# Prompt attention, two heads a step: turned copies ahead of newer exponentials on ScalarE, and the probabilities scaled on GpSimd

## The chip, the cores and the metric

The kernel runs on one core of one Trainium2 chip. The time is that of one execution on the device in microseconds, and the number given for a kernel is the median of its runs.

## The reference, cut to what matters

One step of a decoder with one layer, for 512 prompt tokens and 32 sample tokens. The part that the change touches is the attention of the prompt tokens: 8 heads of latent attention (queries and keys of 96 values, causal) and 8 heads of dilated window attention (64 values). The kernel treats the three dilations of the second kind as one softmax whose scores carry the logarithm of how many windows hold the key. Both kinds then read as follows, per head and per block of 128 queries:

```python
s = q @ k.T * scale + mask          # 128 queries x up to 512 keys
p = exp(s - max(s)); p = p / sum(p) # softmax_stats
o = p @ v
```

The rest of the layer (projections, attention of the sample tokens over cached pages, feed-forward network, gated embedding) stands before and after, and is not changed.

## The kernel before

Everything is laid out with features on the partitions and tokens along the free dimension, in float32. Each engine has a program of its own, written out by hand, and all order between engines comes from semaphores: an engine that waits holds up everything behind it in its program.

**The units.** The prompt attention is a list of 32 units, `units = [(p, i)]`: `p` is a pair of heads (0 to 7; 0 to 3 are latent heads, 4 to 7 window heads) and `i` a block of 128 queries (0 to 3). Unit (p, i) has (i + 1) x 128 keys, so its tiles are 128, 256, 384 and 512 wide, and then it starts again at 128. Each operation on a unit is done for its two heads (z = 0, 1). I call the four units of a pair "the 128, 256, 384 and 512 unit". The eight pairs are numbered 0 to 7.

**The stages of unit n, and who does them.**

1. *Scores*, TensorE, L1012, into one of two PSUM pairs (ps0, ps3).
2. *Masked scores and row maximum*, VectorE, L1273, one instruction and a short read of the accumulator for each head, PSUM to the buffer `probs_of(n, z)` in SBUF; three units have buffers (the names `att` and `prHigh`). Then the negated maximum, L1277 (semaphore `a_nm`).
3. *Exponentials* in place with the row sums, ScalarE, L739, two instructions with an accumulator read each (semaphore `a_e`).
4. *Reciprocal* of the sums, VectorE, L1281, and *scaling* of the probabilities in place by it, VectorE, L1285, twice (semaphore `a_p`).
5. *Turning*: 128x128 blocks are transposed by TensorE through the identity, L1022, into the one PSUM pair ps1 (semaphore `a_t`).
6. *Copy of the turned blocks* for both heads, ps1 to SBUF, one instruction on ScalarE, L748, into `prT` (even units) or a part of `ring` (odd units) (semaphore `a_tc`).
7. *Product with the values*, TensorE, L1033 (semaphore `a_pv`); after a 512 unit VectorE copies the pair's result out, L1291.

**The order of each engine.** At step n TensorE does scores of n, turning of n - 2, product of n - 3. VectorE does stage 2 of n, then stage 4 of n - 1. ScalarE does the exponentials of n and behind them the copy of n - 2. Since ps1 is single, the turning of a unit waits for the copy of the unit before it as well as for its own scaled probabilities. At a few steps other work is put in between: a split of a weight (L752, L1295, steps 6 and 7), clearing and laying out of the sample queries on VectorE (L1297 to L1315, steps 8, 10, 12), and on TensorE the absorbed sample queries (L984, step 24) and the sample tokens' scores among themselves (L993 to L998, step 26) with their read by VectorE.

**GpSimd** has in this stretch only the issue of eight large copies in DRAM (L639, `copy_v`), each held back until the scores of the units 0, 4, 8 and so on are started.

Of the kernel before, what the change touches and what calls it, by code (L numbers as in the profile page):

```python
# [34 lines left out]
P = 128  # L35
# [71 lines left out]
def build(nc, x, cst, gains, win, wqb, wk, wv, wkt, wo, wgu, wdn, wdn2, wpl, plt, pgt, pgl, ck, cv, pt,  # L107
          y, o_lat, o_kr, o_ks, o_vs, o_ck, o_cv):
    with ExitStack() as ctx:
# [18 lines left out]
        def sem(name):  # L128
            return ctx.enter_context(nc.semaphore(name))
# [86 lines left out]
            "krope_spread", "latnew_mm", "latnew_ev", "knew_sq", "knew_ssq"))  # L216
        p_nr = sem("new_scores_read")
        a_s, a_sm, a_e, a_p, a_t, a_tc, a_pv, a_o, a_nm = (sem(n) for n in (
# [409 lines left out]
        def _(pool):  # L628
# [34 lines left out]
            pool.wait_ge(out_s, 80)  # L663
            for k in range(8):
                pool.wait_ge(a_s, 8 * k + 1)
                copy_v(k // 2, k % 2)

# [7 lines left out]
        def _(act):  # L675
# [56 lines left out]

            for n in range(len(units) + LAG_T):
                if n < len(units):
                    w = (units[n][1] + 1) * P
                    act.wait_ge(a_nm, n + 1)
                    for z in range(2):
                        pr = probs_of(n, z)[:, 0:w]
                        last = act.activation(pr, pr, ACT.Exp, bias=st[:, n % 3, NEGM, z:z + 1],  # L739
                                              accum_out=st[:, n % 3, SUM, z:z + 1])  # L740
                    last.then_inc(a_e, 1)
                if n >= LAG_T:
                    m = n - LAG_T
                    w = (units[m][1] + 1) * P
                    act.wait_ge(a_t, m + 1)
                    if m >= 2:
                        act.wait_ge(a_pv, m - 1)
                    act.activation(prT[m % 2][:, :, 0:w], ps[1][:, :, 0:w], ACT.Copy).then_inc(a_tc, 1)  # L748
                if n == 6:
# [442 lines left out]
        def _(v):  # L1192
# [50 lines left out]
            for n in range(len(units) + LAG_PV + 1):  # L1243
# [34 lines left out]
                if 1 <= n <= len(units):  # L1278
                    m = n - 1
                    v.wait_ge(a_e, m + 1)  # L1280
                    link(v.reciprocal(st[:, m % 3, REC1, :], st[:, m % 3, SUM, :]))  # L1281
                    w = (units[m][1] + 1) * P
                    for z in range(2):
                        pr = probs_of(m, z)[:, 0:w]
                        last = v.tensor_scalar(pr, pr, st[:, m % 3, REC1, z:z + 1], None, ALU.mult)  # L1285
                    last.then_inc(a_p, 1)
                if n >= LAG_PV + 1:
# [327 lines left out]
```

## Time and profile before

| | |
|---|---|
| median of 3 runs | 1310.25 us (1310.02 to 1311.48) |
| the profiled execution's own time | 1311.06 us |
| its span in the profile | 1309.3 us |
| TensorE busy | 1204.9 us, 92% |
| VectorE, ScalarE, GpSimd busy | 581.0, 478.6 and 45.7 us |
| the 32 units of prompt attention | about 341.5 to 459.3 us |
| TensorE, VectorE, ScalarE, GpSimd busy in that stretch | 98.7, 74.0, 61.3 and 4.1 us of 117.8 |

In the profile PE is TensorE, PEld its weight loads, DVE VectorE, ACT ScalarE, POOL GpSimd. A float32 matmul stands as several records. The rows give the start and the duration in us, then engine, line, operation, what is written and read, and in brackets how long the engine was idle before it and what ended that. The starts of neighbouring instructions on one engine can be closer together than their durations, because they overlap in the pipeline.

### The profile page before, as it was taken

The numbers are of one execution on the slowest core, as the hardware profiler recorded it, in microseconds if no ns is written. First come the engines' busy times: TensorE is split into PE (matmuls) and PEld (weight loads), VectorE is DVE, ScalarE is ACT, GpSimd is POOL, SyncE is SP. The second block draws the span as 40 slices with busy tenths as digits, with TensorE's granted clock in tenths as the row PEclk, the third lists the DMA queues.
The fourth block names the chain that finished last, engine by engine and source line by source line (L and its number), as shares of the span: only waits on it lengthen the run. The fifth ranks groups of instructions, "written<-read, shape, count | busy, mean of one in ns | idle before, by whom it ended". The sixth has DMA issues, their size and how long they took to land.

```text
span 1309.3 us, 21517 instructions
## 1 busy us (share of the span) xinstructions
PE 1204.9 (92%) x8308; PEld 1007.5 (77%) x8308; DVE 581.0 (44%) x1031; ACT 478.6 (37%) x829; POOL 45.7 (3%) x60
## 2 busy tenths in 40 slices
PE   4999989999988799999999789799999999999698
PEld 3997977333556576666677478799999999999698
DVE  4313321453575576666666364632333233333643
ACT  4223233211355455555555432433321122222332
POOL 0000000232000000000000000000000000000000
PEclk8999999976788799999999879899999999999899
DMA  6675413002348247777777112364662354562122
GB/s 235 237 257 177 139 46 92 10 1 87 129 161 292 71 137 243 245 244 234 247 231 217 48 49 98 113 222 147 216 227 95 136 210 159 208 226 100 43 78 88
DMA packets 68815, 202.66 MB, mean 155 GB/s; under 512 B 7457, under 2 KB 40226, under 8 KB 67394
## 3 DMA queue, kind: packets, MB, share of 16 engines
q1 hardware_dynamic: 66562, 131.74, 30.9%
q0 software_dynamic: 2176, 69.90, 14.9%
q8 instruction: 48, 0.79, 0.2%
q14 instruction: 29, 0.24, 0.1%
HBM read 196.53 MB, written 72.13 MB: 205 GB/s over the span
## 4 chain that ended last, share of the span: by engine, by line
PE 86%; DVE 8%; ACT 3%; issue 2%; DMA 0%; SPq 0%; DVEq 0%; ACTq 0%
PE ps L497 50%; PE ps L1045 13%; PE ps L390 4%; PE ps L401 3%; PE ps L1012 2%; PE ps L413 2%; PE ps L1022 2%; PE ps L1033 2%; DVE R L438 2%; DVE tmp L455 1%; PE ps L1102 1%; PE ps L1096 1%; DVE aLo L356 1%; PE ps L1061 1%; PE ps L936 1%
## 5 line engine op out<-in xcount | busy, mean ns | idle before, releaser
L497 PE MATMUL ps<-aHi,wHi 128*128 128x272 f32 (+1 forms) x1392 | 296.0, 294 | 38.5 <-DVE aLo L356 35.1
L497 PE MATMUL ps<-aHi,wLo 128*128 128x272 f32 (+1 forms) x1392 | 291.8, 292 | 0.0
L497 PE MATMUL ps<-aLo,wHi 128*128 128x272 f32 (+1 forms) x1392 | 291.1, 291 | 0.0
L497 PEld LDWEIGHTS ps<-aHi,wHi 128*128 128x128 f32 (+1 forms) x1392 | 220.0, 189 | 48.9 <-issue 19.5
L369 DVE TENSOR_TENSOR wLo<-ring,wHi 128x1024 fp32r<-128x1024 f32 (+3 forms) x105 | 133.4, 1271 | 211.5 <-ACT wHi L364 211.4
L497 PEld LDWEIGHTS ps<-aLo,wHi 128*128 128x128 f32 (+1 forms) x1392 | 221.2, 190 | 0.0
L497 PEld LDWEIGHTS ps<-aHi,wLo 128*128 128x128 f32 (+1 forms) x1392 | 220.2, 190 | 0.0
L364 ACT ACTIVATE wHi<-ring 128x1024 fp32r<-128x1024 f32 (+3 forms) x105 | 114.5, 1091 | 196.1 <-PE ps L497 196.1
L1328 DVE TENSOR_REDUCE ssq<-att 128x8 f32<-128x512 f32 x128 | 87.4, 683 | 89.1 <-ACT att L767 88.3
L767 ACT ACTIVATE att<-ps 128x512 f32<-128x512 f32 x128 | 76.4, 597 | 114.6 <-PE ps L1045 114.0
L1045 PE MATMUL ps<-wkHi,pgHi 128*128 128x512 f32 x256 | 103.2, 403 | 8.2 <-ACT att L767 7.0
L1045 PE MATMUL ps<-wkHi,pgLo 128*128 128x512 f32 x256 | 100.0, 390 | 0.0
L1045 PE MATMUL ps<-wkLo,pgHi 128*128 128x512 f32 x256 | 99.7, 390 | 0.0
L497 PE MATMUL ps<-hidHi,wLo 128*128 128x272 f32 x352 | 72.9, 288 | 0.0
L497 PE MATMUL ps<-hidHi,wHi 128*128 128x272 f32 x352 | 72.7, 288 | 0.0
L497 PE MATMUL ps<-hidLo,wHi 128*128 128x272 f32 x352 | 72.5, 288 | 0.0
L390 PE MATMUL ps<-sq,C 128*128 128x272 f32 (+5 forms) x196 | 59.3, 456 | 14.1 <-ACT sq L298 14.1
L1045 PEld LDWEIGHTS ps<-wkHi,pgHi 128*128 128x128 f32 x256 | 48.1, 188 | 22.5 <-issue 12.3
L1412 DVE TENSOR_TENSOR sq<-ps,tmp 128x544 f32<-128x544 f32 x22 | 16.0, 725 | 101.3 <-ACT tmp L828 101.3
L390 PEld LDWEIGHTS ps<-sq,C 128*128 128x128 f32 (+5 forms) x196 | 25.6, 146 | 43.0 <-issue 21.7
L1045 PEld LDWEIGHTS ps<-wkHi,pgLo 128*128 128x128 f32 x256 | 48.1, 188 | 10.5
L497 PEld LDWEIGHTS ps<-hidHi,wHi 128*128 128x128 f32 x352 | 55.4, 188 | 0.0
(190 smaller groups left out, 1419.8 us busy)
## 6 DMA issues: line engine op xcount, KB each, us to landing
out_o_cv<-in_cv POOLq DMA_DIRECT2D x16, 2044.0 KB, 8.2
ring<-in_wgu SPq DMA_DIRECT2D x44, 512.0 KB, 3.5
big<-in_pgt SPq DMA_DIRECT2D x128, 144.0 KB, 2.2
big<-in_pgl SPq DMA_DIRECT2D x128, 128.0 KB, 2.4
kv<-in_ck SPq DMA_DIRECT2D x8, 1792.0 KB, 8.0
ring<-in_win SPq DMA_DIRECT2D x21, 512.0 KB, 4.4
kv<-in_cv SPq DMA_DIRECT2D x8, 1024.0 KB, 5.8
kv<-in_cv SPq DMA_DIRECT2D x24, 256.0 KB, 6.2
```

Of the source, the lines that this page charges most:

```text
L364: nc.scalar.activation(wHi[:, u % 2, 0:width], ring[:, u % 2, 0:width], ACT.Copy).then_inc(w_hi, 1)
L369: nc.vector.tensor_tensor(wLo[:, u % 2, 0:width], ring[:, u % 2, 0:width], wHi[:, u % 2, 0:width].bitcast(F32), ALU.subtract).then_inc(w_l ...
L390: last = nc.tensor.matmul(ps[2][out, a, 0:hw], ones, sq[rows, k % 2, a * hw:(a + 1) * hw], start=(j == 0 and t == 0), stop=(j == len(q["sr ...
L401: last = nc.tensor.matmul(spread_pair(g)[rows, a, 0:hw], C[src, C_W + t * P + rows.start:C_W + t * P + rows.stop], R[src, p % 2, a * hw:(a ...
L413: last = nc.tensor.matmul(ps[1][rows, a, 0:HT], C[rows, q["rope"][0] + rows.start:q["rope"][0] + rows.stop], q["dst"][0][:, a * HT:(a + 1) ...
L438: nc.vector.reciprocal(R[rows, p % 2, 0:w], R[rows, p % 2, 0:w]).then_inc(n_rc, 1)
L497: ins = nc.tensor.matmul(pair[rows, a, 0:HT], w[:, c], xx[:, k, a * HT:(a + 1) * HT], start=(k == 0 and z == 0), stop=(k == nk - 1 and z = ...
L767: act.activation(sqK[:, g % 2, :], ps[0][:, g % 2, :], ACT.Square).then_inc(k_sq, 1)
L1012: mm(score_pair(place(n))[:, z, 0:(i + 1) * P], q[:, i * P:(i + 1) * P], k[:, 0:(i + 1) * P], start=True, stop=True).then_inc(a_s, 1)
L1022: last = pe.transpose(ps[1][:, z, j * P:(j + 1) * P], probs_of(m, z)[:, j * P:(j + 1) * P], cm(C_ID))
L1045: last = mm(ps[0][:, g % 2, :], x_[:, g % NBUF, c * P:(c + 1) * P], w_[:, c, :], start=(c == 0 and z == 0), stop=(c == KC - 1 and z == 2))
L1328: v.tensor_reduce(ssq[:, b % 2, t * H:(t + 1) * H], sqK[:, g % 2, :].rearrange("p (h d) -> p h d", h=H), AX.X, ALU.add).then_inc(k_ss, 1)
```

## The change

Two edits, both within the 32 units.

On ScalarE the two blocks of the loop change places: at step n the copy of the turned blocks of unit n - 2 stands in front of the exponentials of unit n, where it stood behind them.

On VectorE the two scaling instructions of stage 4 are gone; the reciprocal stays and now raises a new semaphore `att_recip`. GpSimd scales: it waits for that semaphore, does the two `tensor_scalar` of the unit and raises `a_p`, which TensorE waits for as before. Its eight DRAM copies are spread among the units, each in front of the scaling of a 128 unit.

```diff
@@ gpsimd
-            for k in range(8):
-                pool.wait_ge(a_s, 8 * k + 1)
-                copy_v(k // 2, k % 2)
+            for n in range(len(units)):
+                if n % 4 == 0:
+                    pool.wait_ge(a_s, 2 * n + 1)
+                    copy_v(n // 8, n // 4 % 2)
+                w = (units[n][1] + 1) * P
+                pool.wait_ge(a_rc, n + 1)
+                for z in range(2):
+                    pr = probs_of(n, z)[:, 0:w]
+                    last = pool.tensor_scalar(pr, pr, st[:, n % 3, REC1, z:z + 1], None, ALU.mult)
+                last.then_inc(a_p, 1)
@@ scalar
             for n in range(len(units) + LAG_T):
+                if n >= LAG_T:
+                    m = n - LAG_T
+                    w = (units[m][1] + 1) * P
+                    act.wait_ge(a_t, m + 1)
+                    if m >= 2:
+                        act.wait_ge(a_pv, m - 1)
+                    act.activation(prT[m % 2][:, :, 0:w], ps[1][:, :, 0:w], ACT.Copy).then_inc(a_tc, 1)
                 if n < len(units):
                     w = (units[n][1] + 1) * P
                     act.wait_ge(a_nm, n + 1)
@@
                     last.then_inc(a_e, 1)
-                if n >= LAG_T:
-                    m = n - LAG_T
-                    w = (units[m][1] + 1) * P
-                    act.wait_ge(a_t, m + 1)
-                    if m >= 2:
-                        act.wait_ge(a_pv, m - 1)
-                    act.activation(prT[m % 2][:, :, 0:w], ps[1][:, :, 0:w], ACT.Copy).then_inc(a_tc, 1)
@@ vector
                     v.wait_ge(a_e, m + 1)
-                    link(v.reciprocal(st[:, m % 3, REC1, :], st[:, m % 3, SUM, :]))
-                    w = (units[m][1] + 1) * P
-                    for z in range(2):
-                        pr = probs_of(m, z)[:, 0:w]
-                        last = v.tensor_scalar(pr, pr, st[:, m % 3, REC1, z:z + 1], None, ALU.mult)
-                    last.then_inc(a_p, 1)
+                    v.reciprocal(st[:, m % 3, REC1, :], st[:, m % 3, SUM, :]).then_inc(a_rc, 1)
```

**ScalarE, one pair of heads (pair 3).** The rows are the program's order on that engine, before, and then of the change. L739 (L753 in the change) are the exponentials, x2 for two heads; L748 (L747) the copies of the turned blocks; the last number is the width.

```order
L739 ACTIVATE att,st<-att,st 128x256 x2
L748 ACTIVATE ring<-ps 128x2x512
L739 ACTIVATE prHigh,st<-prHigh,st 128x384 x2
L748 ACTIVATE prT<-ps 128x2x128
L739 ACTIVATE att,st<-att,st 128x512 x2
L748 ACTIVATE ring<-ps 128x2x256
L739 ACTIVATE att,st<-att,st 128x128 x2
```

```order
L747 ACTIVATE ring<-ps 128x2x512
L753 ACTIVATE att,st<-att,st 128x256 x2
L747 ACTIVATE prT<-ps 128x2x128
L753 ACTIVATE prHigh,st<-prHigh,st 128x384 x2
L747 ACTIVATE ring<-ps 128x2x256
L753 ACTIVATE att,st<-att,st 128x512 x2
```

The copy of the 256 unit (`ring<-ps 128x2x256`) stood behind the exponentials of the 512 unit and now stands in front of them; so does each other copy against the exponentials of the unit two further on.

**VectorE, the end of the same pair.** The ISA rows are the masked scores with their maximum, each followed by the read of its accumulator; L1277 (L1284) is the negated maximum, L1281 (L1288) the reciprocal of the unit before it, L1285 the scaling of that unit, L1291 (L1293) the copy of a finished pair. First before, then the change.

```order
L1273 ISA att,st<-ps,C 128x512
L1273 ISA st 128x1
L1277 TENSOR_SCALAR st<-st 128x2
L1281 RECIPROCAL st<-st 128x2
L1285 TENSOR_SCALAR att<-att,st 128x384 x2
L1291 COPY aT<-ps 128x512
```

```order
L1280 ISA att,st<-ps,C 128x512
L1280 ISA st 128x1
L1284 TENSOR_SCALAR st<-st 128x2
L1288 RECIPROCAL st<-st 128x2
L1293 COPY aT<-ps 128x512
```

The scaling is gone; the reciprocal of the 384 unit keeps its place behind the masked scores of the 512 unit.

**GpSimd, the first two pairs.** L639 is the issue of a DRAM copy, L672 the scaling, x2 for the two heads. These are rows of the change; before, the eight L639 stood here in a row with nothing between them.

```order
L639 DMA out_o_cv<-in_cv 32x16352
L672 TENSOR_SCALAR att<-att,st 128x128 x2
L672 TENSOR_SCALAR att<-att,st 128x256 x2
L672 TENSOR_SCALAR prHigh<-prHigh,st 128x384 x2
L672 TENSOR_SCALAR att<-att,st 128x512 x2
L639 DMA out_o_cv<-in_cv 32x16352
L672 TENSOR_SCALAR att<-att,st 128x128 x2
L672 TENSOR_SCALAR prHigh<-prHigh,st 128x256 x2
L672 TENSOR_SCALAR att<-att,st 128x384 x2
```

From the second on, each copy in DRAM now stands behind the scaling of a 512 unit and in front of that of a 128 unit.

## Rows read from the trace of the kernel before

**Rows 1.** The page: the span, and section 1, busy time by engine.
```profile
span 1309.3 us, 21517 instructions
...
PE 1204.9 (92%) x8308; PEld 1007.5 (77%) x8308; DVE 581.0 (44%) x1031; ACT 478.6 (37%) x829; POOL 45.7 (3%) x60
```

**Rows 2.** Busy time by stretch; after each comma busy us, then granted clock, DMA share, GB/s.
```profile
341.50:459.30 117.80, 98.72 (x654) 65.64 (x654) 73.96 (x294) 61.33 (x166) 4.06 (x8) 0.84 0.51 181
350.00:362.00 12.00, 10.59 (x82) 7.21 (x80) 7.53 (x33) 8.11 (x21) 0.53 (x1) 1.00 0.48 175
```

**Rows 3.** Waits in 341.5 to 459.3: total us, times, longest.
```profile
PE ps L1022 <- ACT ring L748: 14.0, 9, 2.4
...
PE ps L1022 <- ACT prT L748: 3.8, 3, 2.9
```

**Rows 4.** Timeline of pair 3 around its 384 and 512 units.
```profile
389.02 0.60 PE L1022 MATMUL ps<-C,att 128*128 128x128 f32 x4
...
389.95 0.17 DVE L1277 TENSOR_SCALAR st<-st 128x2 f32<-128x2 f32 x1
390.03 0.16 DVE L1281 RECIPROCAL st<-st 128x2 f32<-128x2 f32 x1
390.16 0.72 ACT L739 ACTIVATE att<-att,st 128x512 f32<-128x512 f32 x1 [1.77 <-DVE st L1277]
390.22 0.75 DVE L1285 TENSOR_SCALAR prHigh<-prHigh,st 128x384 f32<-128x384 f32 x2
...
391.58 0.57 ACT L748 ACTIVATE ring<-ps 128x512 f32<-128x512 f32 x1
...
392.30 1.46 PE L1022 MATMUL ps<-C,prHigh 128*128 128x128 f32 x6 [1.89 <-ACT ring L748]
...
395.87 1.10 PE L1022 MATMUL ps<-C,att 128*128 128x128 f32 x8
```

**Rows 5.** Timeline: reciprocals, a scaling and turnings of pairs 0, 5, 6 and 7.
```profile
350.34 0.16 DVE L1281 RECIPROCAL st<-st 128x2 f32<-128x2 f32 x1
...
352.61 0.85 PE L1022 MATMUL ps<-C,prHigh 128*128 128x128 f32 x6 [1.41 <-ACT ring L748]
...
420.05 1.54 PE L1022 MATMUL ps<-C,att 128*128 128x128 f32 x6
...
433.02 0.16 DVE L1281 RECIPROCAL st<-st 128x2 f32<-128x2 f32 x1
...
433.21 0.61 DVE L1285 TENSOR_SCALAR att<-att,st 128x256 f32<-128x256 f32 x2
...
434.86 0.63 PE L1022 MATMUL ps<-C,att 128*128 128x128 f32 x4 [2.85 <-ACT prT L748]
...
435.16 0.16 DVE L1281 RECIPROCAL st<-st 128x2 f32<-128x2 f32 x1
...
437.43 1.51 PE L1022 MATMUL ps<-C,prHigh 128*128 128x128 f32 x6 [1.15 <-ACT ring L748]
...
448.98 0.16 DVE L1281 RECIPROCAL st<-st 128x2 f32<-128x2 f32 x1
...
451.25 1.51 PE L1022 MATMUL ps<-C,att 128*128 128x128 f32 x6 [2.15 <-ACT ring L748]
```

**Rows 6.** GpSimd's groups by form: count, then busy us, mean ns, idle before.
```profile
L424 POOL TENSOR_TENSOR tmp<-big,C 96x544 f32<-96x544 f32 x8 | 10.6, 1330 | 32.0 <-DVE big L479 32.0
...
L642 POOL MEMSET vNew<- 128x512 f32 x1 | 0.5, 525 | 0.3 <-POOLq L1593 0.3
...
L643 POOL MEMSET latNew<- 128x256 f32 x1 | 0.3, 312 | 0.0
```

**Rows 7.** Timeline: GpSimd behind VectorE, once undisturbed, once beside a long copy.
```profile
303.47 0.72 DVE L479 TENSOR_TENSOR big<-tmp 96x544 f32<-96x544 f32 x1
...
304.33 1.33 POOL L424 TENSOR_TENSOR tmp<-big,C 96x544 f32<-96x544 f32 x1 [4.59 <-DVE big L479]
...
271.35 2.29 DVE L1230 COPY kv<-big 32x4096 f32<-32x4096 f32 x1
271.47 3.37 POOL L424 TENSOR_TENSOR tmp<-big,C 128x544 f32<-128x544 f32 x1 [2.75 <-DVE big L479]
```

More of the change, by code:

```diff
@@ L216, in build @@
             "krope_spread", "latnew_mm", "latnew_ev", "knew_sq", "knew_ssq"))
-        p_nr = sem("new_scores_read")
+        p_nr, a_rc = sem("new_scores_read"), sem("att_recip")
         a_s, a_sm, a_e, a_p, a_t, a_tc, a_pv, a_o, a_nm = (sem(n) for n in (
```

## The prediction, made before the changed kernel ran

> **What bounds the kernel now.** I read the page's busy times first. TensorE is busy for 1204.9 of 1309.3 us [rows 1], so a change to the other engines can only pay where TensorE stands still. The change lies within the 32 units, so I took the busy times of that stretch: of 117.8 us TensorE is busy for 98.7, which leaves 19.1 us idle, while VectorE (74.0), ScalarE (61.3) and GpSimd (4.1) all have room; the clock granted to TensorE is 0.84 there, against 1.00 in a part of it [rows 2]. Then the waits of the same stretch: 17.8 us of TensorE's idle time stand before the turning (L1022), in 12 waits, and all of them end with a copy of turned blocks on ScalarE (L748) [rows 3]. That is the wait the change goes for.
>
> The timeline of pair 3 shows its making. The turning of the 256 unit is done at 389.62. Its copy could start then, but ScalarE has the exponentials of the 512 unit in front of it, which start at 390.16, when the negated maximum is there, and the copy starts at 391.58. The turning of the 384 unit needs ps1 free and starts at 392.30, after 1.89 us of idle TensorE [rows 4]. Its probabilities were scaled long before: two instructions from 390.22, done at 390.97 [rows 4]. The pattern is rigid: from the start of the 384 unit's reciprocal to the turning of that unit it is 392.30 - 390.03 = 2.27 us in pair 3, and 2.27 in pair 0 (352.61 - 350.34), pair 6 (437.43 - 435.16) and pair 7 (451.25 - 448.98) [rows 4, 5]; pairs 1, 2 and 4 repeat it to the hundredth. Pair 5 has no such wait, as TensorE comes out of the sample queries' work at 420.05 [rows 5].
>
> **The copies moved in front.** With the copy ahead of the exponentials, it runs from about 389.66 to 390.23 (0.57 us) and ps1 is free at 390.4, about when TensorE gets there (392.30 - 1.89 = 390.41) [rows 4]. The exponentials of the 512 unit start at 390.23 instead of 390.16, a loss of 0.07 us that nobody waits for: their turning started at 395.87 [rows 4]. So the copy costs nothing and its wait is gone. What is late next is the scaling of the same unit, done at 390.97 on VectorE: with this edit alone the turning would start at about 391.1, 1.2 us earlier per pair.
>
> **The scaling moved to GpSimd.** The reciprocal of the 384 unit keeps its place behind the masked scores of the 512 unit, so it still starts at 390.03 and takes 0.16 us [rows 4]. To this come: the signal to GpSimd, 0.14 us (VectorE ends at 303.47 + 0.72 = 304.19, GpSimd starts at 304.33 [rows 7]); two multiplications of 384; and the signal to TensorE, which no row shows for GpSimd and which I take as 0.15 us, as from ScalarE (391.58 + 0.57 = 392.15 to 392.30 [rows 4]).
>
> No row shows GpSimd multiplying by a per-partition number. It lies between two forms. Below: a MEMSET, which writes and reads nothing, 0.312 us for 256 and 0.525 us for 512 elements, so 0.42 us for 384. Above: a TENSOR_TENSOR, which reads two operands and writes one, 1.330 us for 544, so 0.94 us for 384 [rows 6]. The scaling reads one operand. I take a third of the way up, 0.59 us, nearer to the MEMSET, because one read can run beside the write and the second of a TENSOR_TENSOR is the one that has no such partner. The pair of heads then takes 1.18 us (VectorE needed 0.75).
>
> For that unknown price the Trainium skill has a page, "GPSIMD Engine Reference". Its section 4.1 calls one-input work on GpSimd roughly line-rate, and section 3.1 gives 769 ns measured for 512 elements in a tight loop of about 1.8 cycles an element. An estimate from the second figure is 0.58 us for 384, and by it the sum below would be the same; at line rate (0.33 us) it would be about 3.6 us better. No row here shows either.
>
> The turning of the 384 unit then starts 0.16 + 0.14 + 1.18 + 0.15 = 1.63 us after the start of the reciprocal, where it was 2.27: 0.64 us earlier in each of the six pairs 0, 1, 2, 3, 4 and 7, together **3.8 us**. Pair 5 gives nothing.
>
> Pair 6 is different, because VectorE is late there: it has read the sample tokens' scores and comes to its units in one go. The turning of the 256 unit waited 2.85 us and started at 434.86 [rows 5]. Without its scaling (0.61 us for two of 256 from 433.21 [rows 5], of which I count 0.57 since neighbours overlap) VectorE reaches the next reciprocal 0.57 us sooner, at 434.59 instead of 435.16, and the turning of the 384 unit follows 1.63 us behind, at 436.22 instead of 437.43: **1.2 us**.
>
> **What else moves.** VectorE loses 64 scalings, some 24 us at half of the 0.75 us in [rows 4]; with 74.0 of 117.8 us busy it waits for the scores elsewhere, so I count this at nothing. GpSimd gets 64 multiplications, at a mean width of 320 about 0.5 us each, 32 us of 118. The 512 unit's scaling starts near 392.1 (ScalarE left its exponentials at 391.58 [rows 4], then the accumulator, reciprocal and signal), takes 2 x 0.77 and is done at 393.6; TensorE comes to it at 395.87 - 0.64 = 395.2. Slack 1.6 us. Each DRAM copy is issued up to 3 us later and takes 0.5 us of GpSimd, in front of the scaling of a 128 unit which is needed only 3 us later; nothing waits for the data. SyncE's queue is not touched.
>
> **The clock.** After about half of these waits TensorE was granted less: six turned blocks take 0.85 us in pair 0 but 1.46 in pair 3 and 1.51 in pairs 6 and 7 [rows 4, 5]. That is 0.6 us on the turning itself; with the product and the scores behind it I estimate 1.5 us an episode. The waits do not vanish (1.89 becomes 1.25), so I count half an episode, **0.7 us**, as gain; the ends are none and four, 0 and 6 us.
>
> **Two engines at one port.** Beside VectorE's copy of 32x4096, which took 2.29 us, a TENSOR_TENSOR on GpSimd that started 0.12 us later took 3.37 us, where eight others took 1.33 [rows 6, 7]: it stood still until the copy was done. The stretch holds work from SBUF to SBUF on VectorE mainly in steps 7 to 12 (L1295 to L1315). I count **0.5 us** as a loss; the ends are nothing and one such hold-up in full, 3.37 - 1.33 = 2 us.
>
> The page "SBUF — State Buffer" of the Trainium skill, in "Who interferes with whom" and the part on its two sides, says that GpSimd shares its one port pair with VectorE, as a lock held for a whole instruction, against VectorE work in a two-port mode or with two SBUF inputs. By that, the trace agrees: 3.37 against 1.33 us. The rule would also let GpSimd hold up the tiny negation L1277, 32 times, if its scaling still runs; no run here shows it.
>
> **Sum.** 3.8 + 1.2 + 0.7 - 0.5 = 5.2 us. The profiled execution took 1311.06 us, so it would take 1305.9. It lies 0.8 us above the median of the runs; from the median, 1310.25 - 5.2 gives **1305.0 us**. A difference of 0.2%, 2.6 us, is about what a measurement of this kernel can tell from none.
>
> **The rivals.**
>
> *Forecast, 0.47*: the wait for the copy becomes a shorter wait for GpSimd, gain 2.6 to 8 us.
>
> *GpSimd near the MEMSET, and the clock stays up, 0.15*: the two instructions take 0.84 us, the turning starts 1.29 us behind the reciprocal, 0.98 us better in six pairs and 1.5 in pair 6, 7.4 us; with two of the low-clock episodes gone, 10.4 us: 1300. For it speaks that pair 0's turning came at full speed behind 1.41 us of idle time; against it, that pair 6's came at 1.51 us behind 1.15 [rows 5].
>
> *No change, 0.20*: GpSimd needs what the TENSOR_TENSOR row says, 0.94 us. The turning starts 0.16 + 0.14 + 1.88 + 0.15 = 2.33 us behind the reciprocal, against 2.27. Six times -0.06 and 0.5 in pair 6 is 0.1 us: 1310. The wait has changed its name and kept its size.
>
> *Slower, 0.18*: GpSimd's multiplication is slower than that row. The mechanism is the same place, the turning of the 384 unit behind two scalings. It decides from 0.91 us for one instruction of 384 on, where the sum 0.45 + 2 x 0.91 reaches 2.27. At 1.2 us it is 2.85 - 2.27 = 0.58 us lost in seven pairs, 4.1 us: 1314. For it speaks that the factor has to be fetched from SBUF for each instruction and that GpSimd's only arithmetic rows are the slow ones; against it, that it reads one long operand less.
>
> **How the numbers follow.** Faster by more than 0.2% are the forecast and the first rival, 0.62; within 0.2%, 0.20; slower, 0.18. The bounds of the unknown price alone give 7.4 us gain to 0.1; with the clock's 6 us the far end is 1297, and with 2 us of port waits and both signals twice as long (seven times 0.3) the other is 1314. The likeliest case by itself spans 1302 to 1307.6. I give 1299 to 1313.
>
> **What would show it.** Right: waits of L1022 on L747 nearly gone; in their place waits on GpSimd's L672, of about 1.2 us, once a pair, before six turned blocks; L672 at 384 wide near 0.6 us; exponentials of the 512 unit starting within 0.1 us of the negated maximum; TensorE idle in the stretch down from 19 to about 14 us. Wrong: L672 at 384 above 0.9 us; L1284 stretched beyond 0.17 us; new waits of TensorE before eight turned blocks (the 512 unit), which would mean that GpSimd has fallen behind by more than the 1.6 us of slack; or the same idle time with the clock lower.

## The result, and the profile after

The changed kernel takes 1325.27 us (median of 4 runs, 1322.58 to 1327.00); the kernel before took 1310.87 beside it. The ratio is 1.0108, 95% interval 1.0089 to 1.0127: slower by 14.4 us, where 5 us less was forecast and 1313 was the end of the range.

The page of the changed kernel, span and busy times (against [rows 1]):

```profile
span 1325.2 us, 21517 instructions
...
PE 1216.6 (92%) x8308; PEld 1013.8 (76%) x8308; DVE 562.4 (42%) x967; ACT 479.1 (36%) x829; POOL 114.3 (9%) x124
```

GpSimd is busy 68.6 us more, where some 32 us of scaling had been counted. TensorE is busy 11.7 us more with the same 8308 instructions: the clock granted to it was lower. The stretch of the 32 units, from TensorE's first scores to its first work on the sample tokens' cached pages (L1052), by windows (columns as in [rows 2]):

```profile
345.22:475.24 130.02, 106.04 (x654) 70.19 (x655) 55.48 (x230) 61.95 (x166) 72.70 (x72) 0.80 0.45 164
```

It is 130.0 us long; the same bounds before are 341.53 and 459.37, 117.8 us. Of the 12.2 us, 7.3 are TensorE's busy time (106.04 against 98.72, clock 0.80 against 0.84 [rows 2]) and 4.9 its idle time (24.0 against 19.1). The stretch also starts 3.7 us later, in a part where nothing differs: the traces of the kernels below start it anywhere from 341 to 349 us, and one and the same kernel (e1 and e11) once at 341.7 and once at 345.2, so I count that part as no effect of the change. And this is one execution of each kernel: the profiled one of the change was the slowest of its four (1327.0 us).

GpSimd's groups by form in the stretch, count, then busy us, mean ns, idle before:

```profile
L672 POOL TENSOR_SCALAR att<-att,st 128x512 f32<-128x512 f32 x12 | 18.6, 1563 | 1.2 <-DVE st L1288 1.2
L672 POOL TENSOR_SCALAR att<-att,st 128x384 f32<-128x384 f32 x10 | 12.6, 1274 | 6.3 <-DVE st L1288 6.3
...
L672 POOL TENSOR_SCALAR prHigh<-prHigh,st 128x384 f32<-128x384 f32 x6 | 7.4, 1244 | 1.7 <-DVE st L1288 1.7
```

One scaling of 384 takes 1.24 to 1.27 us, not 0.59, and longer than a TENSOR_TENSOR of 544 by element [rows 6]. Waits in the stretch (against [rows 3]):

```profile
PE ps L1029 <- POOL att L672: 16.5, 11, 3.1
...
PE ps L1029 <- POOL prHigh L672: 6.1, 6, 2.4
```

The turning is L1029 here. Its waits for ScalarE's copies are gone, all 12 of them, 17.8 us; 17 waits for GpSimd, 22.6 us, stand in their place. Timeline of pair 3 (against [rows 4]):

```profile
397.50 0.17 DVE L1284 TENSOR_SCALAR st<-st 128x2 f32<-128x2 f32 x1
397.58 0.16 DVE L1288 RECIPROCAL st<-st 128x2 f32<-128x2 f32 x1
...
397.71 0.72 ACT L753 ACTIVATE att<-att,st 128x512 f32<-128x512 f32 x1
...
397.83 2.46 POOL L672 TENSOR_SCALAR prHigh<-prHigh,st 128x384 f32<-128x384 f32 x2 [1.47 <-DVE st L1288]
...
398.78 0.32 DVE L1284 TENSOR_SCALAR st<-st 128x2 f32<-128x2 f32 x1
...
400.27 3.10 POOL L672 TENSOR_SCALAR att<-att,st 128x512 f32<-128x512 f32 x2
400.35 0.87 PE L1029 MATMUL ps<-C,prHigh 128*128 128x128 f32 x6 [2.38 <-POOL prHigh L672]
...
403.43 1.71 PE L1029 MATMUL ps<-C,att 128*128 128x128 f32 x8
```

The exponentials of the 512 unit start 0.04 us after the negated maximum: ScalarE's part came as forecast. The turning of the 384 unit starts 400.35 - 397.58 = 2.77 us behind its reciprocal. GpSimd then goes from the 384 unit straight into the 512 unit, 5.56 us in one piece, and the turning of the 512 unit starts as that piece ends, 5.85 us behind the 384 unit's reciprocal. That is as rigid as the 2.27 us were: 2.77 again in pairs 0, 2, 4 and 7, with pairs 0 and 4 shown here; pairs 1 and 6 have 3.08 and 3.01. In five pairs TensorE now waits for GpSimd before the eight turned blocks of the 512 unit too, 0.18 to 0.91 us, and in the trace before it did so in none; the last row is one of them.

```profile
353.26 0.16 DVE L1288 RECIPROCAL st<-st 128x2 f32<-128x2 f32 x1
...
356.03 0.87 PE L1029 MATMUL ps<-C,prHigh 128*128 128x128 f32 x6 [1.05 <-POOL prHigh L672]
...
410.81 0.16 DVE L1288 RECIPROCAL st<-st 128x2 f32<-128x2 f32 x1
...
413.58 0.87 PE L1029 MATMUL ps<-C,att 128*128 128x128 f32 x6 [1.91 <-POOL att L672]
...
416.66 1.97 PE L1029 MATMUL ps<-C,att 128*128 128x128 f32 x8 [0.46 <-POOL att L672]
```

### The profile page after: what moved, and what is told of

The parts are those of the page before. It is cut to its first block, busy times and chain, and to the rows that moved or that the text cites. A ratio compares the mean times of both kernels' runs of the same rounds, so it can differ in the third digit from the quotient of the medians.

```text
span 1325.2 us, 21517 instructions
## 1 busy us (share of the span) xinstructions
PE 1216.6 (92%) x8308; PEld 1013.8 (76%) x8308; DVE 562.4 (42%) x967; ACT 479.1 (36%) x829; POOL 114.3 (9%) x124
## 3 DMA queue, kind: packets, MB, share of 16 engines
q0 software_dynamic: 2176, 69.90, 14.5%
## 4 chain that ended last, share of the span: by engine, by line
PE 85%; DVE 8%; POOL 3%; ACT 2%; issue 1%; DMA 0%; SPq 0%; DVEq 0%; ACTq 0%
PE ps L497 50%; PE ps L1052 13%; PE ps L390 4%; PE ps L401 3%; POOL att L672 2%; PE ps L1019 2%; PE ps L413 2%; DVE R L438 2%; PE ps L1029 1%; PE ps L1040 1%; DVE tmp L455 1%; PE ps L1109 1%; PE ps L1103 1%; PE ps L943 1%; DVE aLo L356 1%
## 5 line engine op out<-in xcount | busy, mean ns | idle before, releaser
L1052 PE MATMUL ps<-wkHi,pgHi 128*128 128x512 f32 x256 | 103.2, 403 | 8.2 <-ACT att L774 7.0
L1052 PE MATMUL ps<-wkHi,pgLo 128*128 128x512 f32 x256 | 99.9, 390 | 0.0
L1052 PE MATMUL ps<-wkLo,pgHi 128*128 128x512 f32 x256 | 99.7, 389 | 0.0
L635 POOL DMA_DIRECT2D out_o_ck<-in_ck x16 | 8.1, 504 | 687.3 <-PE ps L497 687.3
L1052 PEld LDWEIGHTS ps<-wkHi,pgHi 128*128 128x128 f32 x256 | 48.1, 188 | 22.5 <-issue 12.3
L1052 PEld LDWEIGHTS ps<-wkHi,pgLo 128*128 128x128 f32 x256 | 48.1, 188 | 10.5
```

Source lines behind the costliest of these rows:

```text
L1052: last = mm(ps[0][:, g % 2, :], x_[:, g % NBUF, c * P:(c + 1) * P], w_[:, c, :], start=(c == 0 and z == 0), stop=(c == KC - 1 and z == 2))
```

## The experiments

The theory: what costs is how long GpSimd's instruction takes, since TensorE waits for the second of two in a row. The rivals: ScalarE's new order costs; GpSimd's part in the chain costs by itself (signals, or the port it shares with VectorE); TensorE's clock, pulled down by the waits, is the loss. A lower price on GpSimd, with every signal in place, should make the kernel faster; by the first two rivals it should not, and the clock, which hangs on the same waits, has to be moved by itself.

Each ratio is against executions of the kernel before that ran beside it. Their medians were 1310.9 us beside the change, 1312.9 beside e1 to e4, 1314.9 beside e5 to e8, 1311.9 beside e9 to e11 and 1314.1 beside e12 to e14, so kernels of different groups are compared by their ratios, not by their times.

**One edit at a time (e1, e2, e3).** e1 is the kernel before with the two blocks on ScalarE exchanged, and nothing else:

```diff
@@ scalar: what follows the last line here stands behind it as before
+                if n >= LAG_T:
+                    m = n - LAG_T
+                    w = (units[m][1] + 1) * P
+                    act.wait_ge(a_t, m + 1)
+                    if m >= 2:
+                        act.wait_ge(a_pv, m - 1)
+                    act.activation(prT[m % 2][:, :, 0:w], ps[1][:, :, 0:w], ACT.Copy).then_inc(a_tc, 1)
                 if n < len(units):
```

> The copies in front of the exponentials alone; VectorE scales as in the kernel before. Theory A (the reordering helps and the price of GpSimd's scaling, 1.24 to 1.27 us for 384 elements, spoils it): the turning of the 384 unit follows its reciprocal after about 0.16 + 0.75 + 0.15 = 1.1 us instead of 2.27; TensorE's waits for the copies (17.8 us) shrink to some 7 us of waits for VectorE's scaling; 7 to 11 us faster than before. Rival B (the reordering is what costs, because the exponentials now wait behind the turning): slower than before by some us, and ScalarE's exponentials wait for the copies.

Measured: 1296.95 us, ratio 0.9891 (0.9864 to 0.9917). Its window, its waits and its pair 3:

```profile
341.73:440.94 99.21, 87.70 (x655) 57.21 (x655) 73.77 (x294) 62.80 (x166) 4.21 (x8) 0.95 0.58 215
```

```profile
PE ps L1022 <- DVE att L1285: 7.4, 7, 1.9
...
PE ps L1022 <- DVE prHigh L1285: 2.3, 4, 0.8
```

```profile
385.17 0.16 DVE L1281 RECIPROCAL st<-st 128x2 f32<-128x2 f32 x1
...
385.36 0.75 DVE L1285 TENSOR_SCALAR prHigh<-prHigh,st 128x384 f32<-128x384 f32 x2
...
386.16 0.88 PE L1022 MATMUL ps<-C,prHigh 128*128 128x128 f32 x6 [0.62 <-DVE prHigh L1285]
...
388.37 1.09 PE L1022 MATMUL ps<-C,att 128*128 128x128 f32 x8
```

The stretch is 18.6 us shorter than before: idle time 11.5 against 19.1 us and TensorE's busy time 87.7 against 98.7, at a clock of 0.95. The turning of the 384 unit starts 0.99 us behind its reciprocal and that of the 512 unit 3.20. So the reordering is a gain of 14 us, more than the 7 to 11 expected, and by itself larger than anything the prediction had in its sum.

e2 is the change with ScalarE's old order: GpSimd scales, the copies stay behind.

> GpSimd scales, the copies stay behind the exponentials. Theory A: the turning of the 384 unit then follows its reciprocal by the same 2.8 us as in the changed kernel, and all other turnings wait for whichever is later, copy or scaling; 10 to 16 us slower than before, about as slow as the full change. Rival B: near the kernel before, since the full change's loss would be the reordering's.

Measured: 1327.36 us, ratio 1.0113 (1.0084 to 1.0143), as slow as both edits together. The 384 unit's turning is 2.77 us behind again, and it waits for L672 in 17 of 18 cases. With GpSimd last, the earlier copies are worth nothing: two changes whose effects do not add. Its window:

```profile
344.81:469.16 124.35, 97.96 (x655) 64.34 (x655) 55.12 (x230) 61.27 (x166) 72.67 (x72) 0.86 0.48 172
```

The stretch is 5.7 us shorter here than in the change, at a clock of 0.86 and not 0.80, though the waits for GpSimd are as long (24.5 us against 22.6). This trace is the fastest of four executions (1322.53, the others 1326.4 to 1328.7) and that of the change the slowest of its four. With the same waits the clock is thus not the same in every execution, and the split of the 12.2 us above, made from one trace each, is rough.

e3 is the change with the first head's scaling back on VectorE; GpSimd does the second, and TensorE waits for both.

```diff
-                for z in range(2):
-                    pr = probs_of(n, z)[:, 0:w]
-                    last = pool.tensor_scalar(pr, pr, st[:, n % 3, REC1, z:z + 1], None, ALU.mult)
-                last.then_inc(a_p, 1)
+                pr = probs_of(n, 1)[:, 0:w]
+                pool.tensor_scalar(pr, pr, st[:, n % 3, REC1, 1:2], None, ALU.mult).then_inc(a_p2, 1)
```

> Copies in front, VectorE scales the first head of each unit and GpSimd the second. If the time goes by the length of GpSimd's work on the way (theory A), one multiplication of 1.25 us instead of two in a row (2.46 us) puts the turning of the 384 unit at 0.16 + 0.14 + 1.25 + 0.15 = 1.7 us behind the reciprocal: 4 to 8 us faster than before. If what hurts is that GpSimd and VectorE hold each other up at the port (rival C), VectorE's scaling beside GpSimd's takes up to 1.3 us longer in each unit and the gain is gone: within 3 us of the kernel before, or slower, with L1285's counterpart well over 0.42 us for 384.

Measured: 1305.82 us, ratio 0.9942 (0.9924 to 0.9960). GpSimd's groups and VectorE's:

```profile
L671 POOL TENSOR_SCALAR att<-att,st 128x384 f32<-128x384 f32 x5 | 7.4, 1470 | 10.1 <-DVE st L1287 10.1
```

```profile
L1291 DVE TENSOR_SCALAR att<-att,st 128x384 f32<-128x384 f32 x5 | 2.1, 420 | 0.2
```

```profile
394.01 0.16 DVE L1287 RECIPROCAL st<-st 128x2 f32<-128x2 f32 x1
...
395.83 0.85 PE L1028 MATMUL ps<-C,prHigh 128*128 128x128 f32 x6 [1.44 <-POOL prHigh L671]
```

The turning starts 1.82 us behind (1.7 expected). GpSimd's instruction, started beside VectorE's, is about 0.2 us longer than in the change, and VectorE's is not longer than before. The gain of 8 us is at the top of the 4 to 8 expected.

**The price itself (e4, e5, e6).** e4 is the kernel before with GpSimd's forms one after the other in its first, idle microseconds, each behind the end of the one before.

> The kernel before, with a dozen operations on GpSimd alone put into its idle first microseconds, each waited for: the scaling with a factor from SBUF at 128, 256, 384 and 512, with a constant at 128, 384 and 512, a plain copy at 384 and 512, a product of two tensors at 256, 384 and 512. If the fetch of the factor is what makes it slow, the constant form is shorter by a fixed 0.2 us or more; if the form itself is slow for each element, both have the slope of 2.5 ns an element, steeper than the product of two tensors (0.94 us for 384 by the kernel before).

GpSimd's groups by form, in the first 16 us (L655 has its factor in SBUF, L658 a constant, L667 multiplies a tile by itself). These rows are all that I read from it:

```profile
L655 POOL TENSOR_SCALAR vNew<-vNew,latNew 128x384 f32<-128x384 f32 x1 | 1.2, 1242 | 0.1
L658 POOL TENSOR_SCALAR vNew<-vNew 128x384 f32<-128x384 f32 x1 | 1.2, 1172 | 0.1
L667 POOL TENSOR_TENSOR vNew<-vNew 128x384 f32<-128x384 f32 x1 | 0.8, 825 | 0.1
...
L661 POOL COPY vNew<-vNew 128x512 f32<-128x512 f32 x1 | 0.6, 612 | 0.1
...
L661 POOL COPY vNew<-vNew 128x384 f32<-128x384 f32 x1 | 0.5, 502 | 0.1
...
L668 POOL MEMSET vNew<- 128x512 f32 x1 | 0.5, 525 | 0.1
```

With no other work beside it the scaling of 384 takes 1242 ns: the price in the change is its own, not contention. Fetching the factor is 70 ns of it. A copy is near the MEMSET, as had been assumed of one-operand work; the TENSOR_SCALAR is not of that kind, and slower than the product of two tensors.

e5 is the change with that product: the reciprocal is read again for each element.

```diff
-                    last = pool.tensor_scalar(pr, pr, st[:, n % 3, REC1, z:z + 1], None, ALU.mult)
+                    last = pool.tensor_tensor(pr, pr, st[:, n % 3, REC1, z:z + 1].broadcast_to([P, w]), ALU.mult)
```

> The change with one thing different: GpSimd multiplies with TENSOR_TENSOR by the reciprocal repeated along the row, in place of TENSOR_SCALAR; the same result. In the run of the forms TENSOR_TENSOR took 825 ns at 384 and 1041 ns at 512 where TENSOR_SCALAR took 1242 and 1562. If the length of GpSimd's instruction is what costs, the turning of the 384 unit starts 0.16 + 0.14 + 2 x 0.83 + 0.15 = 2.1 us behind its reciprocal (2.27 before, 2.77 at the first measured turning of the change), the 512 unit's scaling ends about 1 us sooner, and the kernel takes about what the one before took: 1308 to 1314 us, 11 to 19 us less than the change. If GpSimd in the chain costs by itself (signals, a port), whatever its instruction takes, it stays above 1319.

Measured: 1308.28 us, ratio 0.9951 (0.9932 to 0.9970). Its timeline in pair 3:

```profile
390.66 0.16 DVE L1288 RECIPROCAL st<-st 128x2 f32<-128x2 f32 x1
...
390.90 1.61 POOL L672 TENSOR_TENSOR prHigh<-prHigh,st 128x384 f32<-128x384 f32 x2 [2.11 <-DVE st L1288]
...
391.86 0.67 DVE L1284 TENSOR_SCALAR st<-st 128x2 f32<-128x2 f32 x1
...
392.56 0.66 PE L1029 MATMUL ps<-C,prHigh 128*128 128x128 f32 x4 [1.52 <-POOL prHigh L672]
```

The turning comes 1.90 us behind (2.1 expected), and the kernel is 6 us faster than before, where about the same time had been expected. One other form of the same multiplication turns 1.1% slower into 0.5% faster. VectorE's negation, 0.17 us alone, ends here (392.53) with the TENSOR_TENSOR that it ran beside (392.51).

e6 is the change with `tensor_copy(pr, pr)` in that place: the scaling by the reciprocal is left out, all waits and signals stay.

> The change with GpSimd copying each tile onto itself in place of scaling it: the scaling by the reciprocal is left out, every wait and signal stays. In the run of the forms the copy took 502 ns at 384 and 612 at 512, near the 0.59 us at 384 with which the prediction's sum was made. If only the price was wrong in that sum, the kernel takes 1299 to 1306 us (5 us better than before, and a few more if TensorE's clock goes up with the shorter waits), and the stretch of the 32 units is 105 to 113 us long. If the sum was wrong elsewhere too (the signals, GpSimd's queue with the DRAM copies in it), it is within 2 us of the kernel before or above it.

Measured: 1302.07 us, ratio 0.9901 (0.9882 to 0.9920), so 13 us less than before.

```profile
388.35 0.16 DVE L1288 RECIPROCAL st<-st 128x2 f32<-128x2 f32 x1
...
388.57 0.96 POOL L672 COPY prHigh<-prHigh 128x384 f32<-128x384 f32 x2 [2.55 <-DVE st L1288]
...
389.58 0.88 PE L1029 MATMUL ps<-C,prHigh 128*128 128x128 f32 x6 [0.85 <-POOL prHigh L672]
```

A copy of 384 takes 0.51 to 0.62 us, and the turning starts 1.23 us behind. This is the change at about the price that the prediction assumed; the gain is more than twice its sum. Not all of that is the clock: two copies take 0.96 us here and not 1.18, and the two signals 0.11 and not 0.29, so the turning is 0.4 us sooner than the 1.63 of the sum.

**The port (e7).** e1, with GpSimd multiplying a tile of zeros by 1.0 beside it, at the times and widths of the change; nobody waits for it within the units.

```diff
+                    v.sem_inc(a_rc, 1)    # VectorE, behind its reciprocal
@@ gpsimd
+                    pool.tensor_scalar(vNew[:, 0:w], vNew[:, 0:w], 1.0, None, ALU.mult).then_inc(a_scr, 1)
+                    pool.wait_ge(a_scr, 2 * n + z + 1)
```

> The version with the copies in front and the scaling on VectorE, and beside it GpSimd multiplies a tile of zeros that nobody reads (vNew) by 1.0, at the same times and widths as in the change, each after the one before it is done; TensorE waits for the last of them only after the units. If the two engines hold each other up at the port, VectorE's scaling grows beyond 0.42 us at 384, its negation beyond 0.17 us, and half or more of that version's gain of 1.1% is gone. If GpSimd costs only because TensorE waits for its result, VectorE's rows keep their lengths and the time is that of the version with the copies in front, 1295 to 1302 us.

Measured: 1306.76 us, ratio 0.9929 (0.9911 to 0.9948): 0.4% of e1's 1.1% is gone, uncertain by 0.3%. VectorE's scaling of 384, in this kernel and then in e1:

```profile
L1293 DVE TENSOR_SCALAR att<-att,st 128x384 f32<-128x384 f32 x10 | 5.0, 540 | 0.8 <-DVE st L1288 0.8
```

```profile
L1285 DVE TENSOR_SCALAR att<-att,st 128x384 f32<-128x384 f32 x10 | 3.7, 417 | 0.2
```

```profile
395.06 0.16 DVE L1288 RECIPROCAL st<-st 128x2 f32<-128x2 f32 x1
...
395.38 0.99 DVE L1293 TENSOR_SCALAR prHigh<-prHigh,st 128x384 f32<-128x384 f32 x2 [0.16 <-DVE st L1288]
...
396.43 0.77 PE L1028 MATMUL ps<-C,prHigh 128*128 128x128 f32 x5 [0.98 <-DVE prHigh L1293]
```

Work on GpSimd that nobody waits for makes VectorE's scaling 20 to 30% longer and the turning 0.38 us later (1.37 us behind), of which 0.13 is the added signal (VectorE's scaling starts 0.32 us behind the reciprocal instead of 0.19). The result lies between the two outcomes expected: VectorE's rows grow, but less than half of the gain is gone. The two engines do hold each other up, and of the 2.2% between e1 and the change it explains a small part at most: the change has no scaling on VectorE, GpSimd's 384 takes there what it takes alone (1.24 to 1.27 against 1.24 us), and what is left for the port in it no run isolates.

**The clock (e8, e14, e13, e10, e9, e12).** e8 and e14 are the change with 12 more transposes of the identity on TensorE, once a pair, ahead of its wait for the scaled 384 unit, into columns that nobody reads then. In e8 they had to wait for VectorE to copy an output away; in e14, whose edit is shown, they start at once.

```diff
+                    if n % 4 == 0:
+                        for _ in range(12):
+                            pe.transpose(ps[2][:, (n // 4 - 1) % 2, 3 * P:4 * P], cm(C_ID), cm(C_ID))
                     pe.wait_ge(a_p, m + 1)
```

> The change, with 12 extra transposes of the identity put on TensorE ahead of its wait for the 384 unit's scaled probabilities, once a pair, into a bank that nobody reads. They fill 0.9 us of that wait at full speed and 2 to 3 us at half. If TensorE's idle time is what lowers its clock and the clock carries 8 of the 12 us lost, the granted clock of the stretch goes up from 0.80 and the stretch gets shorter than 130 us, to 122 to 127. If the clock does not hang on these short waits, the clock stays at 0.80 and the stretch is as long or, where the filler outlasts the wait at the low clock, 1 to 5 us longer.

Measured: 1319.79 us, ratio 1.0037 (1.0023 to 1.0051). More work on the busiest engine made the kernel faster: the stretch fell from 130.0 to 120.7 us, its clock rose from 0.80 to 0.94. This is no accident of one trace: over the whole execution the clock was 0.945 to 0.946 in all 5 executions of e8, 0.943 to 0.947 in the 12 of e14, and 0.933 to 0.938 in the 4 of the change.

```profile
345.47:466.18 120.71, 102.05 (x750) 70.25 (x751) 55.27 (x230) 61.95 (x166) 72.71 (x72) 0.94 0.49 177
```

> The change with the same 12 transposes that start at once. With the flawed filler the stretch was 120.7 us, work proper about 90 us at 0.94 against 106 at 0.80. If the clock is the larger part of the loss, the stretch is 115 to 120 us and the kernel takes 1311 to 1317, within 0.3% of before; the rest, 22 us of waits for GpSimd, stays. If the waits are the larger part, it is above 1319.

Measured: 1320.10 us, ratio 1.0042 (1.0027 to 1.0058), the outcome in which the waits are the larger part. Its stretch, and then that of e13, which is the kernel before with the same 12 transposes:

```profile
344.52:466.50 121.98, 103.86 (x751) 71.82 (x751) 55.25 (x230) 61.95 (x166) 72.68 (x72) 0.91 0.49 175
```

```profile
345.36:457.91 112.55, 100.29 (x751) 70.36 (x751) 73.79 (x294) 61.35 (x166) 4.05 (x8) 0.93 0.52 190
```

> The kernel before with 12 extra transposes ahead of the 384 unit's turning that start at once; the waits for ScalarE's copies stay. With the flawed filler TensorE's work proper in the stretch was 100.0 - 14.5 = 85.5 us at a clock of 0.94, against 98.7 at 0.84 without. So if the clock falls because of these waits, the stretch is 117.8 - 13 + what the filler sticks out (12 take 1.5 us, the wait is 1.4 to 2.2): 104 to 109 us, and the kernel takes 1297 to 1303. If the higher clock is eaten up again by later waits of TensorE for the other engines (they do not run faster), it is 1303 to 1310.

Measured: 1309.65 us, ratio 0.9979 (0.9960 to 0.9998), the weaker of the two outcomes: TensorE's own work shrank by 12.9 us (100.3 less 14.5 of filler, against 98.7), but the stretch by 5.3 only. TensorE cannot pass the engines that it waits for: the turning of the 384 unit is 2.27 us behind its reciprocal again in pairs 1, 3, 4 and 7. And in pair 5, where there was no wait, and pair 6, where it was short, the filler sticks out: 5.94 and 3.99 us behind against 3.81 and 2.27.

The pair e13 and e14 tells the two parts of the loss. With nearly the same clock in both, the change is still 1.0042 - 0.9979 = 0.63% slower, of 1.08% without filler. So some 8 of the 14 us are lateness as such, and some 6 us come through the clock. The first figure is uncertain by about 0.25% (3 us), the second, a difference of two such figures, by 0.3% (4 us). The stretches of the single traces give 9.4 (121.98 less 112.55) of 12.2 us, which leaves 3 for the clock. That lateness is the larger part is likely, the exact split is open.

e10 and e9 were meant to be e13 and e12, with the flawed place of the filler:

> The kernel before with the same 12 extra transposes at the same place as in the change with filler; every other engine keeps its order. The waits for the copies of turned blocks stay, 1.4 to 2.4 us each; the clock of the stretch was 0.84 and TensorE's work in it 98.7 us, against 87.7 at 0.95 in the version with the copies in front. If the clock falls because TensorE stands still in these waits, the clock goes to 0.93 or more, the work proper shrinks by some 8 us and the kernel takes 1302 to 1307 us (0.3 to 0.7% less than before). If only shorter waits help and the clock is an effect of something else, it stays within 2 us of before or is slower by what the filler sticks out.

> The copies in front, scaling on VectorE, and 8 extra transposes of the identity on TensorE ahead of its wait for the 384 unit's scaled probabilities, once a pair. Twelve such transposes took 1.53 us at full speed, so 8 take 1.0 us of a wait that is about 1.1 us long in that version. The granted clock of its stretch is 0.95 already. If TensorE's pauses set the clock it goes to 0.97 or more, worth at most 2 or 3 us: 1294 to 1297 us where the version without them takes 1297. If the filler does not fit into the wait everywhere, it costs up to 8 x 0.5 us and the two are equal or it is 1 to 4 us slower.

Measured: 1310.97 us, ratio 0.9985 (0.9966 to 1.0003) for e10, not told from the kernel before although the clock of its stretch rose to 0.94; and 1310.21 us, 0.9976 (0.9958 to 0.9994) for e9, where 1294 to 1301 us had been expected. The waits of e9 name the flaw:

```profile
PE ps L1021 <- DVE aT L1296: 9.4, 6, 2.2
```

VectorE copies the output out only behind the scaling of the 384 unit, so the filler started when its place was already over. e12 has it mended:

> The copies in front, scaling on VectorE, and 8 extra transposes ahead of the 384 unit's turning, now in columns that nobody needs yet, so they start at once. With the wait for VectorE's copy of the output gone (9.4 us, 6 times, before), what is left is 8 x 1.0 us of filler in waits of about 1.1 us: 1294 to 1299 us, the stretch 97 to 101 us, as without filler. If filler costs for another reason, it stays near 1310.

Measured: 1297.79 us, ratio 0.9880 (0.9856 to 0.9904), beside e1 once more:

> The version with the copies in front once more, beside the two with filler on one chip. As measured first: 1.1% faster than before (interval 0.8 to 1.4%), 1295 to 1302 us, the stretch 99 to 103 us long with the clock at 0.93 to 0.95.

Measured: 1297.30 us, ratio 0.9878 (0.9854 to 0.9903). The version with the copies in front repeats, and filler adds nothing to it: its clock was 0.94 already.

All kernels in order of how far the 384 unit's turning stands behind its reciprocal in pair 3:

| kernel | one scaling of 384, on | turning behind | stretch | clock | TensorE busy, idle | ratio |
|---|---|---|---|---|---|---|
| e1, copies in front | 0.42 us, VectorE | 0.99 us | 99.2 us | 0.95 | 87.7, 11.5 us | 0.9891 |
| e6, GpSimd copies | 0.51 to 0.62 | 1.23 | 102.6 | 0.90 | 91.9, 10.6 | 0.9901 |
| e7, e1 with GpSimd beside | 0.50 to 0.54, VectorE | 1.37 | 109.6 | 0.89 | 93.8, 15.8 | 0.9929 |
| e3, one head each | 1.47, GpSimd | 1.82 | 108.0 | 0.91 | 91.5, 16.5 | 0.9942 |
| e5, TENSOR_TENSOR | 0.83 to 0.92 | 1.90 | 109.7 | 0.89 | 93.1, 16.5 | 0.9951 |
| before | 0.42, VectorE | 2.27 | 117.8 | 0.84 | 98.7, 19.1 | 1 |
| the change | 1.24 to 1.27 | 2.77 | 130.0 | 0.80 | 106.0, 24.0 | 1.0108 |
| e2, copies behind | 1.24 to 1.27 | 2.77 | 124.4 | 0.86 | 98.0, 26.4 | 1.0113 |

The last column follows the third closely, whichever engine sets it. From 0.99 to 2.77 us it goes up by 2.2%, 28 us, so one microsecond at this place, which comes eight times, goes with about 16 us and not 8; later turnings of the other units and the clock are in that. Stretch, clock and busy time are of one execution each, the ratio of all.

## Why the prediction was wrong

**The step that failed is GpSimd's price**, "I take a third of the way up, 0.59 us". The reason given, that one-operand work lies between a MEMSET and a TENSOR_TENSOR, holds for a copy (0.50 us at 384) and not for a TENSOR_SCALAR, 1.24 us, which lies outside both bounds. Nothing in the trace before showed that form, and rows of other operations were taken as bounds. That the same chain at 0.5 to 0.6 us gives 0.9901 (e6), and at 0.83 to 0.92 us 0.9951 (e5), shows that this step turned the sign. By an estimate, 0.59 us with the measured signals would have put the turning 0.16 + 0.09 + 1.18 + 0.06 = 1.49 us behind, between e6 and e3, which are 1.0 and 0.6% faster than before: at its own price the forecast would have had the right sign and too small a size.

The Trainium skill, "GPSIMD Engine Reference", section 4.1, calls one-input work roughly line-rate, and its section 3.1 gives 769 ns for 512 elements in a tight loop of about 1.8 cycles an element. For this form the trace does not agree: 1.56 us for 512 elements (e4). A COPY of 512 stays below the second figure, with 0.61 us.

**The rival named it and priced it too low.** The slower rival had the place and the point of decision: 0.91 us by its signals, 0.98 by the measured ones, which are 0.09 us from VectorE to GpSimd and 0.06 to TensorE instead of 0.14 and 0.15. Its price at 1.2 us was 0.58 us a pair, 4.1 in all, 1314 (with pair 6 credited by the 0.57 us that the forecast's own sum gave it, 3.5). The 384 unit's turning is indeed 0.50 us later in five pairs and 0.81 and 0.74 in pairs 1 and 6, 4.05 us together: as far as it went, the rival was right. What it lacked:

- *Pair 5.* It "gives nothing", and it lost 1.72 us: 5.53 us behind its reciprocal instead of 3.81. Why is not shown.
- *The 512 unit.* "Slack 1.6 us" was worked out at 0.59 us a scaling and not again at 1.2. There the two units on GpSimd are one piece, and TensorE waits for it before the 512 unit's eight blocks in five pairs, 2.5 us in all. The 512 unit's turning comes 6.20, 5.85 and 5.85 us behind the 384 unit's reciprocal in pairs 0, 3 and 7, where before it was 4.60, 5.84 and 4.78, and 3.2 in e1's pair 3.
- *The clock.* It was counted as 0.7 us of gain with ends at nothing and 6 us of gain, never as a loss. It belonged to each rival with its sign: longer waits pull it down, here from 0.84 to 0.80 in the two traces, and filling them in the change (e8, e14) gave 0.7% back.

**The copies moved in front: right, and under-used.** "1.2 us earlier per pair" with this edit alone; it is 1.28 (2.27 less 0.99). Seven times 1.2 is 8.4 us, and with the clock it is 14 to 16: the prediction had the 1.2 us and a sum for both edits of 5.2, less than the one edit gives by its own figure, and drew nothing from that. At 0.59 us each, moving the scaling put 0.43 us of work and a signal more into the chain, for a counted 24 us of relief to an engine that TensorE's waits did not name.

**The clock's size: wrong in the good cases too.** e6 has 7 us less TensorE time in the stretch and e1 11, where the estimate was 0.7. Half an episode (one such stretch) of 1.5 us was counted, since 1.25 us of wait would remain. Between e13 and before only the filling of these waits differs, and 12.9 us of TensorE's work go away: stretches of low clock were more and longer than the six turned blocks and their neighbours showed.

**The port: it is there, but works the other way round.** 0.5 us was counted for GpSimd held up by VectorE's copies of the sample queries. In the change it is those copies and the negation that are held up, while GpSimd's rows of 384 take 1.24 to 1.27 us, alone 1.24. Beside GpSimd's scaling the negation L1284 took 0.32 us instead of 0.17 (pair 3 above; mean 194 ns against 170) and ended at 399.10, as the first of GpSimd's two instructions did (397.83 and half of 2.46 is 399.06), and the small copies of the sample queries 328 ns against 175. With VectorE's scaling in the chain it costs about 0.4%, the added signal included (e7). The Trainium skill's rule in "SBUF — State Buffer", "Who interferes with whom", let this be expected of L1284, and the trace agrees: 0.32 against 0.17 us.

**VectorE's relief at nothing, and the DRAM copies hidden: nothing speaks against them.** VectorE is busy 55.5 instead of 74.0 us of the stretch, and e2, which has this relief and the old order, is slower than before. In e6 the DRAM copies stand in GpSimd's queue as in the change, and it is 1% faster.

The version that beats both kernels is e1: 1.1 and 1.2% faster than before in two sets of runs, and 2.1 to 2.3% faster than the change.

## What to carry to other kernels

Price an offload by the very form of instruction on the very engine, run once in an idle microsecond; another operation's row is no bound. When a rival's price is tried, run the whole chain again at that price, the next unit's slack included, and give the clock the sign of the waits. And price each edit of a change alone: where one of them already clears the wait, the other may do no more than add to the chain.

## What the hardware showed that was not expected

GpSimd's TENSOR_SCALAR in float32, alone (e4), takes 0.60, 0.93, 1.24 and 1.56 us for 128, 256, 384 and 512 elements, 2.5 ns for each element more, against 0.83 and 1.04 us for a TENSOR_TENSOR (a tile by itself, or in e5 by a column repeated) and 0.50 and 0.61 for a COPY of 384 and 512: the form with fewer long operands is the slower one, with a constant as with a factor from SBUF.

In this stretch the clock granted to TensorE hangs on pauses of 1 to 3 us: 12 useless transposes ahead of eight turnings raised it from 0.80 to 0.91 and 0.94 and made the changed kernel 0.7% faster. It does not hang on them alone: e2, with the same waits as the change, had 0.86 in its trace.
